# Five stages of an encoder block in one block of engine programs instead of five with barriers between

## What is computed

```python
hn = rmsnorm(h, attn_norm)
q_g, k_g, v_g, c_q, c_kv, k_r, gates = split(hn @ w_in)      # 512, 128, 128, 384, 256, 32, 2048 columns
q_g, k_g = rope2d(rmsnorm(q_g)), rope2d(rmsnorm(k_g))        # 8 query heads, 2 key heads of 64
o_g = softmax(q_g @ k_g.T / 8) @ v_g
q_m = rmsnorm(c_q) @ w_uq                                    # 8 heads of 64 + 32 (rope)
k_nope, v_m = split(rmsnorm(c_kv) @ w_ukv)
o_m = softmax((qn @ k_nope.T + qr @ rope2d(k_r).T) / sqrt(96)) @ v_m
mixed = sigmoid(g_a) * (o_g @ w_o_gqa) + sigmoid(g_b) * (o_m @ w_o_mla)
h = h + mixed @ w_out
h = h + expert_choice_ffn(rmsnorm(h, ffn_norm))              # 16 experts, each takes its 130 best rows
y = rmsnorm(h, final_norm)[:, 16:]
```

## Time and profile before

| | |
|---|---|
| median of three runs | 3171.61 us |
| the profiled execution's own time | 3172.54 us |
| its span, first to last instruction | 3170.7 us |
| mean granted TensorE clock | 0.950 |
| TensorE matmuls (PE) | 2844.9 us busy, 90% |
| VectorE (DVE) | 1868.2 us, 59% |
| ScalarE (ACT) | 1485.2 us, 47% |
| GpSimd (POOL) | 669.5 us, 21% |

### The profile page before, as it was taken

One profiled execution on the slowest core, in us unless ns is written; L12 is line 12 of the kernel. 1 busy time (PEld: TensorE's weight loads), 2 busy tenths in 40 slices (PEclk: granted clock), 3 DMA queues, 4 the chain that ended last, 5 costly groups with the idle time before them and its releaser, 6 DMA issues. The chain is left out here.

```text
span 3170.7 us, 56367 instructions
## 1 busy us (share of the span) xinstructions
PE 2844.9 (90%) x20018; PEld 2631.8 (83%) x20018; DVE 1868.2 (59%) x3149; ACT 1485.2 (47%) x2690; POOL 669.5 (21%) x1237
## 2 busy tenths in 40 slices
PE   5999685899999999999699999989952999999991
PEld 4888575799998888888699999978832999999991
DVE  4887653788887777777233343423355555555544
ACT  3333232788887777777222232312221445454432
POOL 0000000344444333334000000000021233333321
PEclk8999898899999999999899999989975999999995
DMA  5657499121121323333847475456643788888857
GB/s 166 181 166 206 113 286 303 32 69 38 53 50 48 97 71 92 79 91 89 267 129 227 127 220 147 140 159 187 192 137 78 189 205 203 199 204 201 205 115 243
DMA packets 597519, 476.05 MB, mean 150 GB/s; under 512 B 57744, under 2 KB 537664, under 8 KB 597360
## 3 DMA queue, kind: packets, MB, share of 16 engines
q1 hardware_dynamic: 578976, 439.54, 49.2%
q0 software_dynamic: 12288, 34.10, 6.0%
q10 hardware_dynamic: 6096, 0.40, 0.1%
HBM read 320.31 MB, written 153.62 MB: 149 GB/s over the span
## 5 line engine op out<-in xcount | busy, mean ns | idle before, releaser
L1223 PE MATMUL t_s_ps<-t_k,t_q 96*128 96x512 f32 (+2 forms) x1392 | 379.6, 403 | 22.3 <-POOL t_ident L119 20.3
L1660 PE MATMUL c_acc<-c_tokens,c_w_hi 128*128 128x260 f32 x2048 | 374.3, 284 | 26.2 <-DVE c_w_lo L1731 25.9
L1408 DVE TENSOR_REDUCE t_peak<-t_s_ps 128x1 f32<-128x1024 f32 (+2 forms) x276 | 336.8, 1221 | 83.0 <-PE t_s_ps L1223 82.7
L1430 DVE TENSOR_TENSOR t_pt_lo<-t_tp,t_pt_hi 128x512 fp32r<-128x512 f32 x552 | 336.3, 650 | 24.9 <-ACT t_pt_hi L1354 24.5
L1660 PEld LDWEIGHTS c_acc<-c_tokens,c_w_hi 128*128 128x128 f32 x2048 | 317.7, 190 | 26.7 <-issue 26.7
L1354 ACT CAST t_pt_hi<-t_tp 128x512 fp32r<-128x512 f32 x552 | 284.7, 565 | 110.6 <-PE t_tp L1251 109.6
L1324 ACT ACTIVATE t_probs<-t_s_ps,t_bias 128x1024 f32<-128x1024 f32 (+2 forms) x276 | 308.5, 1118 | 22.2 <-POOL t_bias L1485 7.2
L1223 PEld LDWEIGHTS t_s_ps<-t_k,t_q 96*128 96x128 f32 (+2 forms) x1392 | 244.2, 183 | 67.7 <-POOL t_ident L119 20.4
L2188 PE MATMUL e_gu<-e_x_hi,w_hi 128*128 128x260 f32 x1024 | 293.6, 287 | 0.9 <-DVE e_x_lo L2331 0.9
L1660 PE MATMUL c_acc<-c_tokens,c_w_lo 128*128 128x260 f32 x1024 | 290.3, 283 | 0.0
L2188 PE MATMUL e_gu<-e_x_lo,w_hi 128*128 128x260 f32 x1024 | 289.6, 283 | 0.0
(11 more groups left out here) (231 smaller groups left out, 6363.2 us busy)
## 6 DMA issues: line engine op xcount, KB each, us to landing
c_raw<-in_w_in SPq DMA_DIRECT2D x64, 512.0 KB, 5.5
w_raw<-in_w_gate SPq DMA_DIRECT2D x64, 512.0 KB, 6.6
w_raw<-in_w_up SPq DMA_DIRECT2D x64, 512.0 KB, 8.0
w_raw<-in_w_down SPq DMA_DIRECT2D x64, 512.0 KB, 4.5
c_tokens<-hn_t SPq DMA_DIRECT2D x16, 1040.0 KB, 9.7
c_tokens<-o_t SPq DMA_DIRECT2D x32, 520.0 KB, 7.4
r_mt<-mix_t SPq DMA_DIRECT2D x32, 512.0 KB, 5.2
t_k<-mk_t SPq DMA_DIRECT2D x32, 390.0 KB, 5.1
```

Source lines behind the costliest of these rows:

```text
L1223: ins = pe.matmul(s_ps[0:r, n % 2, half * 512:(half + 1) * 512], query(n, a), key(n, c, half * 512, (half + 1) * 512), start=(at == 0), st ...
L1408: dve.tensor_reduce(peak[0:r, b % 2, i:i + 1], s_ps[0:r, n % 2, :], AX_X, ALU.max).then_inc(peak_done, 1)
L1430: dve.tensor_tensor(pt_lo[span], tp[:, f % RING, :].rearrange("p (t n) -> p t n", t=4)[:, :, 0:r], pt_hi[span].bitcast(F32), ALU.subtract) ...
L1660: pe.matmul(acc[:, b, mixer, 0:W], w[:, parity, mixer, k, :], tokens[t % 2][:, part, k, cols], start=(k == 0 and at == 0), stop=(k == DK - ...
```

## The change

The five stages share one block and one identity matrix; each function now takes the block and hands on what marks its end, as (semaphore, value) pairs, on which the next stage's engines wait where they first touch something of the stage before. The clearing of semaphores moves behind the residual stage. Unit 0 of attention is loaded in the latents' steps 1 and 2, unit 1 in the first block of attention. Four pairs of the mix's token loads go to single blocks of attention, 20, 16, 12 and 8 before the last unit; the last unit's first block holds the rest and the weight pieces. The residual's first mixed tile is loaded in the mix's last unit, and x gets semaphores of its own. In the diff a line of "..." marks what is left out: signatures, the removed `block = ...` and identity matrices of each stage.

```diff
...
+class ResidualLoads:
+    def __init__(self, nc, late):
+        self.mt0 = late.at(0, "r_mt0", [P, 2, DK, P], F32R)
+        self.loaded = [nc.alloc_semaphore("r_loaded0"), nc.alloc_semaphore("r_loaded1")]
+    def load_mixed(self, sp, scr, g):
+        for part in range(2):
+            sp.dma_start(self.mt0[:, part, :, :].bitcast(F32), scr["mix_t"][part, g, :, :, 0:P]).then_inc(self.loaded[0], 16)
...
+    return dict(evacuated=(tp_lo, fill("kcT", N - 1, 0)[0] + 1), values_split=(v_split, N),
+                inputs_stored=[(hn_stored[0], 32 * ((N + 1) // 2 + 1)), (hn_stored[1], 32 * (N // 2))])
...
# latents
-                if isinstance(j, int) and N - 3 <= j < N - 1:
-                    u = j - (N - 3)
-                    first_units.load_qk(sp, scr, u)
+                if isinstance(j, int) and j == 1:
+                    first_units.load_qk(sp, scr, 0)
+                if isinstance(j, int) and j == 2:
                     sp.wait_ge(pads_ready, 2)
-                    first_units.load_v(sp, scr, u)
+                    first_units.load_v(sp, scr, 0)
...
         @block.tensor
         def _(pe):
-            pe.wait_ge(ident_ready, 2)
+            pe.wait_ge(*projected["evacuated"])
...
         @block.scalar
         def _(act):
+            act.wait_ge(*projected["values_split"])
...
+                    if isinstance(s, int) and s == 0:
+                        for landed, value in projected["inputs_stored"]:
+                            act.wait_ge(landed, value)
...
-            identity_matrix(pool, ident, ident_ready)
+            pool.wait_ge(*projected["evacuated"])
...
+    done = (tp_lo, fill("mkT", N - 1, 0)[0] + 1)
...
# attention
-                sp.wait_ge(s_filled, first_chunk[u - 1])
-                sp.wait_ge(tp_filled, number["meta_scores", first_block[u - 1] - 1] + 1)
+                if u >= 2:
+                    sp.wait_ge(s_filled, first_chunk[u - 1])
+                    sp.wait_ge(tp_filled, number["meta_scores", first_block[u - 1] - 1] + 1)
...
-                starts = first_block[u] == b and 2 <= u + 1 < len(units)
+                starts = first_block[u] == b and u + 1 < len(units)
...
+                for at in range(2 * mix_loads.NB):
+                    if b == last_unit - 4 * (at + 2):
+                        mix_loads.load_tokens(sp, scr, mix_loads.first, 0, at // 2, at % 2)
                 if b == last_unit:
-                    for nb in range(2):
-                        for mixer in range(2):
-                            mix_loads.load_tokens(sp, scr, mix_loads.first, 0, nb, mixer)
-                if b == last_unit + 1:
+                    for gone in (last_unit - 2, last_unit - 1):
+                        sp.wait_ge(stored[gone % 2], stored_after[gone])
+                    for nb in range(mix_loads.NB):
+                        mix_loads.load_tokens(sp, scr, mix_loads.first, 0, nb, 2)
                     sp.wait_ge(s_filled, first_chunk[len(units) - 1])
                     sp.wait_ge(tp_filled, number["meta_scores", last_unit - 1] + 1)
                     for mixer in range(2):
                         mix_loads.load_piece(sp, io, 0, mixer)
-                    for gone in (last_unit - 2, last_unit - 1):
-                        sp.wait_ge(stored[gone % 2], stored_after[gone])
-                    for nb in range(2):
-                        mix_loads.load_tokens(sp, scr, mix_loads.first, 0, nb, 2)
...
             def meta_scores(b):
...
+                if b == 0:
+                    pe.wait_ge(*latents_done)
...
+    return dict(summed=(o_summed, BLOCKS), scaled_rows=(tp_act, number["scales", BLOCKS - 1] + 1), split=(out_done, BLOCKS),
+                stored=[(stored[p], store_total[p]) for p in range(2)])
...
# mix
                         load_out(m)
+                        if m == DK - 1:
+                            sp.wait_ge(piece_lo, 2 * DK * PASSES)
+                            sp.wait_ge(stored, 32 * DK)
+                            residual_loads.load_mixed(sp, scr, 0)
...
+                    if t == 0 and isinstance(m, int) and m == 0 and b == 1:
+                        pe.wait_ge(*attended["summed"])
+                        pe.wait_ge(*attended["scaled_rows"])
...
             split_pieces(0, 0, 0)
+            for landed, value in attended["stored"]:
+                act.wait_ge(landed, value)
...
             split_pieces(0, 0, 0)
+            dve.wait_ge(*attended["split"])
+            for landed, value in attended["stored"]:
+                dve.wait_ge(landed, value)
...
+    return dict(products=(prod_done, NB * DK * PASSES), first_products=(prod_done, NB * DK * PASSES - 1),
+                out_weights=(out_split_lo, DK))
...
# residual
-        mt = sb("mt", [P, 2, 2, DK, P], F32R)
+        mt = [loads.mt0, sb("mt1", [P, 2, DK, P], F32R)]
...
-                    for part in range(2):
-                        sp.dma_start(mt[:, g, part, :, :].bitcast(F32), scr["mix_t"][part, g, :, :, cols])\
-                            .then_inc(loaded[g], 16)
+                    if not (isinstance(s, int) and s == 0):
+                        for part in range(2):
+                            sp.dma_start(mt[g][:, part, :, :].bitcast(F32), scr["mix_t"][part, g, :, :, cols])\
+                                .then_inc(loaded[g], 16)
                     sp.dma_start(x[:, g, :], io["x_prompt" if g == 0 else "x_sample"][0, cols, :])\
-                        .then_inc(loaded[g], 16)
+                        .then_inc(x_loaded[g], 16)
...
-            pe.wait_ge(ident_ready, 2)
+            pe.wait_ge(*mixed_done["out_weights"])
+            pe.wait_ge(*mixed_done["first_products"])
             def body(j, parity):
+                if isinstance(j, int) and j == 1:
+                    pe.wait_ge(*mixed_done["products"])
...
                     dve.wait_ge(acc_filled, s + 1)
+                    dve.wait_ge(x_loaded[g], 16 * (tile_index(s, g) + 1) + (16 if isinstance(s, int) and s == N - 1 else 0))
...
# build
-    with ExitStack() as ctx:
+    with nc.cleanup_on_exit(), ExitStack() as ctx:
+        block = ctx.enter_context(nc.Block())
+        ident = ctx.enter_context(nc.sbuf_tensor("ident", [P, P], F32))
...
-        with nc.cleanup_on_exit():
-            project(nc, io, scr, early, ahead)
+        projected = project(nc, io, scr, block, ident, early, ahead)
...
```

More of the change, by code:

```diff
@@ L354, in split_product, with project @@
     return ins
-def project(nc, io, scr, early, ahead):
+def project(nc, io, scr, block, ident, early, ahead):
     N = STEPS
@@ L412, in project @@
         qkv_stored = sem("qkv_stored")
-        block = ctx.enter_context(nc.Block())
         fill = Fills((("hnT", 1), ("qT", -1), ("kcT", -1)), 1, 1)
@@ L739, in _, with latents @@
             steps(pool, body, 1, 1)
-def latents(nc, io, scr, early, ahead, first_units, pads_ready):
+    return dict(evacuated=(tp_lo, fill("kcT", N - 1, 0)[0] + 1), values_split=(v_split, N),
+                inputs_stored=[(hn_stored[0], 32 * ((N + 1) // 2 + 1)), (hn_stored[1], 32 * (N // 2))])
+def latents(nc, io, scr, block, ident, early, ahead, projected, first_units, pads_ready):
     N = STEPS
@@ L986, in _, with attention @@
             steps(pool, body, 1, 1)
+    done = (tp_lo, fill("mkT", N - 1, 0)[0] + 1)
     landed = [(sem_of[p], each * ((N + 1) // 2 + 1 if p == 0 else N // 2))
               for sem_of, each in ((stored, STORES), (mv_stored, 16)) for p in range(2)]
-    return landed
-def attention(nc, io, scr, held, pads_ready, latents_landed, mix_loads):
+    return done, landed
+def attention(nc, io, scr, block, ident, held, latents_done, latents_landed, mix_loads):
     MIXERS = 2
@@ L1141, in load_v @@
             def load_v(u):
[L1143 removed]
+                if u >= 2:
+                    sp.wait_ge(o_filled, first_block[u - 1])
                 held.load_v(sp, scr, u)
@@ L1556, in _, with mix @@
                 split_lo(b)
-def mix(nc, io, scr, loads, w_out):
+    return dict(summed=(o_summed, BLOCKS), scaled_rows=(tp_act, number["scales", BLOCKS - 1] + 1), split=(out_done, BLOCKS),
+                stored=[(stored[p], store_total[p]) for p in range(2)])
+def mix(nc, io, scr, block, loads, attended, w_out, residual_loads):
     WIDE, NB, W, OK, HALF_K = loads.WIDE, loads.NB, loads.W, loads.OK, loads.HALF_K
@@ L1769, in _, with residual @@
                     body(DK - 1, 1, True)
-def residual(nc, io, scr, w_out):
+    return dict(products=(prod_done, NB * DK * PASSES), first_products=(prod_done, NB * DK * PASSES - 1),
+                out_weights=(out_split_lo, DK))
+def residual(nc, io, scr, block, ident, w_out, loads, mixed_done):
     N = STEPS
@@ L2521, in build @@
     scr = scratch_tensors(nc)
-    with ExitStack() as ctx:
+    with nc.cleanup_on_exit(), ExitStack() as ctx:
+        block = ctx.enter_context(nc.Block())
+        ident = ctx.enter_context(nc.sbuf_tensor("ident", [P, P], F32))
         early = Region(nc, ctx, "early", EARLY)
```

(17 more changed lines are left out.)

28 lines of the change are left out of this document (8 added, 20 removed).

## The result

The changed kernel takes **3133.83 us** (median of four runs, 3131.98 to 3135.12) against 3170.93 for the kernel before (four runs, 3169.54 to 3172.42): ratio 0.9882, 95% interval 0.9865 to 0.9900. The forecast was 3119.4, range 3106 to 3133: faster, as said, but 14 us less so than said, and 0.8 us outside the range. The profiled execution took 3131.98 us with a span of 3129.7 us, so the two profiled spans differ by 41.0 us where the forecast had 52.2. These 11.2 us are what has to be found; the medians are 37.1 apart because the profiled execution of the changed kernel was the fastest of its four, and that of the kernel before (3172.54) lies above the highest of its runs.

The account below looks back on a forecast made before the run. Most stages were taken as bound by matmuls, the latents by transfers, with gains only where TensorE waits. 22.2 + 21.5 + 9.2 - 0.7 = 52.2 us off the profiled 3172.5, median 0.9 lower: 3119.4 us, range 3106 to 3133.

Parts of the forecast that it names:

- unit 0's place in the latents: Latents, steps 1 and 2: about 2.5 us of its 10.2 fill free capacity; the other 7.7 push the stage back.
- Project to latents: First boundary: ScalarE's weight cast starts at 366.4 instead of 370.14, 3.8 us gained.
- Latents to attention: Second boundary: first attention copy at 544.9 instead of 567.09, 22.2 us gained, the first boundary's 3.8 included.
- Unit 1's removal: Latents: unit 1's loads now go after the stage, taking 10.2 us off it.
- The four stores: Between last latent split and first attention copy: ScalarE's own four store issues take 6.0 us and are late next.
- the four early pairs: Late attention: token pairs of 1 to 2 MB, at most 6 us of queue, covered by GpSimd's two blocks.
- Attention to mix: Third boundary: first cast of the mix at 1508, TensorE at 1511.4 against 1532.94, 21.5 us gained.
- Mix to residual: Last boundary: TensorE starts the residual at 2094.4, after the last weight split, instead of 2103.60; 9.2 us gained.
- Clearing: End of the residual: semaphore clearing moved there from the first boundary, charged 0.7 us.
- Rival 1: Boundaries: the clock does not fall in the shortened pauses, giving 3110 us; chance 0.15, together with quick ScalarE issues.
- rival 3: Start of attention: the clock stays low, the gain is gone or the kernel ends at 3180 us; chance 0.03.
- Rival 2: Latents or mix: unit 0 (10 us) or the pieces (8 us) late; 3129 with one, 3137 both; chance 0.20.

Follow-up runs that it names:

- e3: The changed kernel with unit 0's loads back in the latents' step 14, unit 1 still in attention's first block; 3131.44 us.
- e9: e1 with unit 0 of attention loaded behind the last latent stores instead of in the latents' second and third step; 3131.21 us.
- e4: The changed kernel with ScalarE's four last latent stores issued by SyncE instead; 3128.32 us.
- e1: The changed kernel with one 2.1 MB pair of token loads moved from block 73 to block 72 of attention; 3121.88 us.
- e2: e1 with another 2.1 MB pair moved from block 81 to 82, right ahead of a unit's loads; 3132.59 us.
- e6: e1 with a 1.06 MB pair moved from block 77 to 76, right ahead of a unit's loads; 3126.74 us.
- e8: The changed kernel with the residual's first mixed tile loaded with x after the mix's stores landed, not in the mix's last unit; 3142.21 us.

## Why the forecast fell short

Two terms of the sum failed, unit 0's place in the latents (2.5 us counted, none seen) and attention, where nothing was counted and 8.0 us were lost. What was said of the pauses at the boundaries themselves held within 1 us each.

- **Project to latents, 3.8 us: right.** ScalarE's last store ends at 367.12 and its first cast starts at 367.21. The projection itself ended 0.7 us later in this execution, so the gain reads 2.9 us in the trace and 3.7 with that taken off. TensorE's first matmul was due at 368.3 and came at 369.1. Its wait there is 6.9 to 7.0 us in all eleven kernels without this barrier and 10.7 us in both that have it.
- **Latents to attention, 22.2 us: the term of unit 0 was mis-sized; 18.2 measured.** "About 2.5 us of free capacity are filled, and the other 7.7 us push the rest": nothing was won by it. The 0.49 was the mean over a step from 0.04 to 0.95, and the load came at the step. With 10.2 us charged, and the first low split 1.3 us later than forecast (0.7 of it the projection's), the last split is due at 542.6; it ended at 542.7. That agreement is closer than traces 4 us apart allow, so it is no proof by itself. e3 is the test: with unit 0 at its old place the latents take 153.6 us against 153.5, and the time is 2.4 us shorter, not 2.5 longer (the intervals of the two ratios overlap, so the shorter time itself isn't shown). e9 puts the bytes at 8.1 to 8.5 us. The rule of the Trainium skill cited in the forecast (DMA: Bandwidth & Descriptors, queues, rings and completion order) gave 2.5 us less than my sum; the 542.7 agrees with it, within that scatter. Unit 1's removal gave 10.0 us (163.6 to e3's 153.6), forecast 10.2. The four stores, 6.0 forecast, took 6.1 and were, as said, late next; e4 takes them out and wins 4.0 at the copy.
- **Attention, nothing forecast: 8.0 us lost.** The step that failed is the sentence on the four early pairs: "Their cover is the two blocks that GpSimd has until it wants the same output buffer again". It counted the stores behind the pairs and left out the unit loads behind them. The last of this unit's queries, issued at 1307.15, were wanted at 1314.3, where TensorE stopped: 7.2 us for a landing whose median is 6.7 and which took 13.0 here. Even without the 1.3 us in which SyncE issued the pair, under 2 us were to spare (2.4 us as e1's trace has it, where the slower query load takes 7.0 us: issued at 1303.90, wanted at 1313.34). When a unit's queries are issued and when they are first used could be read in the trace before. e1 removes the loss, e2 makes it elsewhere, e6 halves the wait with half the bytes.
- **Attention to mix, 21.5 us: right,** 21.2 measured. The piece is 0.8 us late, forecast 0.5.
- **Mix to residual, 9.2 us: right,** 9.3 by the pause (13.8 to 4.5), and the stage itself was 0.7 us shorter.
- **Clearing, 0.7 us: 0.4 measured,** within what a single trace tells.
- **The rivals.** Rival 1 did not come: the granted clock fell in each shortened pause, to 0.50 in attention's first stretch (552 to 556) and in the mix's (1500 to 1505), and 0.60 in the residual's (2062 to 2066). Nor did rival 3, since it stood at 1.00 again from 560. Rival 2, a load that is late, is the nearest to what happened, but its price fits by luck. It had 10 us for unit 0 in the latents and 8 us for the mix's pieces, so 3129 with one and 3137 with both; what came is 2.5 us at the first place, next to nothing at the second (0.8 us late against the 0.5 forecast), and 8.0 us at a place that it didn't name, a unit's queries in attention.

```profile
552.00:556.00 4.00, 3.25 (x12) 2.89 (x13) 1.25 (x2) 1.95 (x5) 0.29 (x1) 0.50 0.99 299
...
560.00:564.00 4.00, 3.68 (x26) 2.71 (x25) 3.97 (x8) 3.77 (x9) 0.78 (x4) 1.00 0.82 228
1500.00:1505.00 5.00, 3.51 (x16) 3.54 (x17) 3.27 (x2) 1.47 (x1) 1.19 (x2) 0.50 0.24 75
...
2062.00:2066.00 4.00, 3.83 (x10) 3.06 (x11) 0.12 (x1) 0.00 (x0) 0.00 (x0) 0.60 0.54 159
```

What stays open: why kernels with the same loads there differ by up to 4 us in the latents. No kernel opens only the first boundary, so what its 3.7 us are worth in time isn't shown. And no kernel puts the pair of tokens on another engine's queue at the same moment, so the runs don't tell whether the unit's loads were late because they stood behind the pair in SyncE's order or because both shared the same transfer engines.

## What to carry to other kernels

When a prefetch moves into a quieter stretch, list everything that is issued behind it on the same queue and compare each one's time from issue to use with its landing time: the slack was some 2 us here, and bytes in front cost their own transfer time once it is used up. A block earlier 2.1 MB cost nothing, and neither did 1.06 MB right behind a unit's loads in the same block. Cut a stretch of half-used transfers into pieces before calling it free, and remember that in this stage, whose transfers were full, moving bytes won nothing and taking them out did. Much of what looks like a barrier's cost is what it waits for: here two thirds of the largest gain came from the loads' order with the barrier still in place.

## What was not expected of the hardware

A short stop of TensorE in attention cost some 3 us beyond itself: waits of 2.4, 4.6, 5.4, 5.6, 5.7 and 5.9 us (e6, e2, e3, e8, e4 and the changed kernel) lengthened attention by 5.8, 7.6, 8.6, 8.5, 8.8 and 8.5 us against 939.5. The traces show the reason as 4.7 to 7.0 us of work at a granted clock of 0.50 after each, worked out from the means of the stretches behind it. Such a stop is thus priced at 1.4 to 1.7 times its length, the shortest at 2.4 times.

It isn't so for every short stop. In the latents of the kernel before, a wait of 2.2 us left the clock at 1.00, and one of 2.7 us, at 511.17, was followed by a mean of 0.61 over 4 us, 1.6 us of slower work. What decides it, no run here shows; the clock has to be read behind each stop.

```profile
482.58 0.58 PE L350 MATMUL l_acc<-l_uq_hi,l_lat 128*128 128x384 f32 x2 [2.18 <-DMA l_lat<-lat_t]
...
482.00:486.00 4.00, 3.42 (x19) 3.44 (x20) 3.26 (x6) 0.53 (x1) 0.00 (x0) 1.00 1.04 274
...
512.00:516.00 4.00, 4.00 (x17) 4.00 (x16) 1.20 (x4) 0.00 (x0) 0.00 (x0) 0.61 1.10 275
```
